# Expert weights in 2 MB units with 16 KB runs per partition, eight slots in place of sixteen

## What is computed

```python
def moe_ffn(h, router_w, router_b, w_gate_up, b_gate_up, w_down, b_down):
    logits = (hf @ router_w + router_b).astype(jnp.float32)
    top_vals, top_idx = lax.top_k(logits, TOP_K)          # 4 of 32 experts
    gates = jax.nn.softmax(top_vals, axis=-1)
    ...
    def run_block(args):
        tok, e = args
        xb = h_pad[tok]
        gu = xb @ w_gate_up[e] + b_gate_up[e]             # 1024 -> 2048
        gate = jnp.minimum(gu[:, :EXPERT_DIM], SWIGLU_LIMIT)
        up = jnp.clip(gu[:, EXPERT_DIM:], -SWIGLU_LIMIT, SWIGLU_LIMIT)
        act = gate * jax.nn.sigmoid(SWIGLU_ALPHA * gate) * (up + 1.0)
        return act @ w_down[e] + b_down[e]                # 1024 -> 1024
    ...
    y = jax.ops.segment_sum(out, slot_token, num_segments=n_tok + 1)[:n_tok]
```

## Time and profile before

| | us |
|---|---|
| median of 3 runs | 1174.46 (1172.85 to 1175.27) |
| span of the profiled execution, first to last instruction | 1171.9 |
| PE busy in the span | 1062.5 (91%) |
| first of the 16 pairs: first addition into the output | 286.06 |
| last of the 16 pairs: first addition into the output | 1165.98 |
| DMA engines from 300 us to 1140 us | busy throughout, 418 GB/s |

### The profile page before, as it was taken

How to read it: one execution, slowest core, us unless ns; L and a number is a source line. 1 busy time by engine, 2 the same in 40 slices (tenths; PEclk the granted TensorE clock), 3 DMA queues, 4 the chain that set the end, 5 groups by cost and what they waited for, 6 DMA issues and landing times.

```text
span 1171.9 us, 11745 instructions
## 1 busy us (share of the span) xinstructions
PE 1062.5 (91%) x4392; PEld 409.5 (35%) x4392; DVE 300.4 (26%) x585; ACT 166.6 (14%) x272; POOL 5.2 (0%) x12
## 2 busy tenths in 40 slices
PE   5999999899998989898989898989898989898987
PEld 2444544433333333333333333333333333233322
DVE  1563021322122222222222212121212121222212
ACT  2123200311111111111111101010101010111110
POOL 1000000000000000000000000000000000000000
PEclk9999999899999999999999999999999999999999
DMA  9942322798999999999999999999999999999996
GB/s 329 348 139 98 131 105 110 276 414 352 414 423 413 422 414 421 414 422 415 422 414 422 415 422 415 421 415 422 416 419 417 421 418 418 418 419 418 417 420 255
DMA packets 84019, 430.36 MB, mean 367 GB/s; under 512 B 7953, under 2 KB 8081, under 8 KB 51233
## 3 DMA queue, kind: packets, MB, share of 16 engines
q1 hardware_dynamic: 83456, 428.20, 90.0%
q0 software_dynamic: 544, 1.90, 0.5%
HBM read 429.03 MB, written 1.05 MB: 367 GB/s over the span
## 4 chain that ended last, share of the span: by engine, by line
PE 63%; SPq 25%; issue 3%; DMA 3%; DVE 3%; ACT 1%; DVEq 0%; PEldq 0%
SPq L262 25%; PE bank L1029 24%; PE bank L1083 13%; PE bank L826 9%; PE bank L848 5%; PE bank L992 4%; PE bank L1098 3%; DMA ring<-w_gate_up_dram 2%; PE bank L998 2%; DVE big L758 2%; DMA ring<-w_in_dram 1%; ACT big L419 1%; PE bank L801 1%; DVE big L776 1%; ACT big L436 1%
## 5 line engine op out<-in xcount | busy, mean ns | idle before, releaser
L1029 PE MATMUL bank<-ring,big 128*64 128x512 f32 x1536 | 342.6, 596 | 8.9 <-PE bank L1029 5.6
L1029 PEld LDWEIGHTS bank<-ring,big 128*64 128x64 f32 x1536 | 107.2, 137 | 229.1 <-issue 212.8
L1083 PE MATMUL bank<-ring,big 128*64 128x512 f32 x768 | 168.3, 594 | 0.0
L826 PE MATMUL bank<-ring,hT 128*128 128x512 f32 (+1 forms) x256 | 105.3, 570 | 4.6 <-DMA ring<-w_in_dram 4.0
L751 DVE COPY big<-bank 128x512 f32<-128x512 f32 x32 | 22.1, 691 | 304.7 <-PEq L1042 177.5
L1083 PEld LDWEIGHTS bank<-ring,big 128*64 128x64 f32 x768 | 53.8, 137 | 103.1 <-issue 103.1
L992 PE MATMUL bank<-xn,kqT 128*128 128x512 f32 x136 | 65.9, 629 | 19.0 <-DVE big L758 19.0
L436 ACT ACTIVATE big<-bank 128x512 f32<-128x512 f32 x32 | 19.1, 597 | 410.2 <-PEq L1042 270.3
L998 PE MATMUL bank<-consts,big 128*128 128x128 f32 x392 | 52.8, 277 | 26.8 <-ACT big L436 14.1
L1098 PE MATMUL bank<-big,kqT 128*128 128x512 f32 x128 | 61.8, 615 | 15.3 <-DVE big L776 15.3
L826 PEld LDWEIGHTS bank<-ring,hT 128*128 128x128 f32 x256 | 47.0, 196 | 60.0 <-issue 60.0
(11 more groups left out here) (216 smaller groups left out, 699.7 us busy)
## 6 DMA issues: line engine op xcount, KB each, us to landing
ring<-w_gate_up_dram SPq DMA_DIRECT2D x192, 1024.0 KB, 19.6
ring<-w_down_dram SPq DMA_DIRECT2D x96, 1024.0 KB, 20.5
siga<-w_gate_up_dram SPq DMA_DIRECT2D x16, 1024.0 KB, 22.1
sigp<-w_gate_up_dram SPq DMA_DIRECT2D x16, 1024.0 KB, 24.1
qo<-w_gate_up_dram SPq DMA_DIRECT2D x16, 1024.0 KB, 23.4
hT<-w_gate_up_dram SPq DMA_DIRECT2D x16, 1024.0 KB, 24.8
ring<-w_in_dram SPq DMA_DIRECT2D x14, 1024.0 KB, 14.4
siga<-w_down_dram SPq DMA_DIRECT2D x8, 1024.0 KB, 21.3
```

The costliest lines, as they stand in the source:

```text
L826: ins = MM(bank[PAIR_BANKS[j % 3][b]][:, 0:n], hT[:, kc, b * P:b * P + P], w[:, k, :], start=kc == 0, stop=kc == KC - 1)
L1029: ins = MM(bank[2 * e + h][T * g:T * g + T, :], xgT[:, k, T * e:T * e + T], ring[s][:, D * g + 512 * h:D * g + 512 * h + 512], start=k == ...
L1083: ins = MM(bank[4 + h][T * e:T * e + T, :], actT[:, c, T * e:T * e + T], v3(ring[ws[e]][:, :], 2)[:, k, 512 * h:512 * h + 512], start=c == ...
```

## The change

A unit becomes 2 MB, with one run of 16 KB for each partition: two neighbouring rows of gate/up, or four of down. A pair has 12 units, 8 of gate/up and 4 of down. There are 8 slots with the same bytes in all: six of the `ring`, one that joins `siga` and `sigp` (`sg`), one that joins `hT` and `qo` (`hq`). The front part uses the ring as 12 halves with their own semaphores, as before; the loop's slots get new ones (`slot_in`, `slot_used`).

With `k` rows to a partition, partition `p` now holds rows `k p` to `k p + k - 1`. So the operands that meet the weights are rearranged: the transposes of the gathered tokens (`X`) take every second column of their source, and those of the gate/up result (`TA`, `TB`) every fourth. The two tables on partitions are rearranged once, on the chip: a new function `turn_tables` on PE between `projection(0)` and `projection(1)` multiplies them with columns of the identity into two PSUM banks, and DVE copies them from there to `bgu` and a new tile `g2`; PE waits for that copy.

```diff
-RING = 12
-EXTRA = 4
+RING = 6
+EXTRA = 2
 SLOTS = RING + EXTRA
+HALVES = 2 * RING
-PAIR_UNITS = 24
-UW = 2048
+PAIR_UNITS = 12
+UW = 4096
+HW = 2048
...
-        ring += [siga_t, sigp_t, qo_t, hT_t]
+        half = [ring[s // 2][:, HW * (s % 2):HW * (s % 2) + HW] for s in range(HALVES)]
+        ring += [sg_t, hq_t]
...
-            if u < 16:
-                row = (2 * p + u // 8) * D + (u % 8) * P
-                return w_gu[bass.ds(row, P), :]
-            j = u - 16
-            row = (2 * p + j % 2) * D + (j // 2) * 2 * P
-            return w_dn[bass.ds(row, 2 * P), :].rearrange("(k p) n -> p k n", p=P)
+            if u < 8:
+                row = (2 * p + u // 4) * D + (u % 4) * 2 * P
+                return w_gu[bass.ds(row, 2 * P), :].rearrange("(p k) n -> p (k n)", k=2)
+            j = u - 8
+            row = (2 * p + j % 2) * D + (j // 2) * 4 * P
+            return w_dn[bass.ds(row, 4 * P), :].rearrange("(p k) n -> p (k n)", k=4)
...
                 if s < RING:
-                    sp.wait_ge(unit_used[s], PRE_TURNS)
+                    sp.wait_ge(unit_used[2 * s], PRE_TURNS)
+                    sp.wait_ge(unit_used[2 * s + 1], PRE_TURNS)
                 elif s == RING:
                     sp.wait_ge(t_ready, TJ_M + 4)
-                elif s == RING + 2:
-                    sp.wait_ge(job_ready, 2 * (BJ_WA + NB))
-                elif s == RING + 3:
+                else:
                     sp.wait_ge(t_ready, TJ_R[1] + 1)
                 pair_unit(0, s)
...
+            dve.wait_ge(turned_ready, 1)
+            V.tensor_copy(bgu_t[:, :].rearrange("p (e j k g) -> p e j k g", e=E, j=2, k=4),
+                          bank[4][:, :].rearrange("p (k e j g) -> p e j k g", k=4, e=E, j=2)).then_inc(turned_read, 1)
+            V.tensor_copy(g2_t[:, :].rearrange("p (j k) -> p j k", k=2), bank[5][:, 0:KC].rearrange("p (k j) -> p j k", k=2)).then_inc(turned_read, 1)
+            dve.wait_ge(turned_read, 2)
...
+            def turn_tables():
+                pe.wait_ge(bgu_in, 16)
+                pe.wait_ge(cols_in, 16)
+                for k in range(4):
+                    for g in range(4):
+                        MM(bank[4][32 * g:32 * g + 32, k * P:k * P + P], ident[:, k::4],
+                           bgu_t[:, :].rearrange("p (e j c g) -> p e j c g", e=E, j=2, c=4)[:, :, :, g, :],
+                           start=True, stop=True)
+                for k in range(2):
+                    for g in range(2):
+                        ins = MM(bank[5][64 * g:64 * g + 64, 4 * k:4 * k + 4], ident[:, k::2], cols[:, P_G2 + g:P_G2 + g + 7:2],
+                                 start=True, stop=True)
+                ins.then_inc(turned_ready, 1)
+                pe.wait_ge(turned_read, 2)
+
             for j in range(4):
                 projection(j)
+                if j == 0:
+                    turn_tables()
...
-            def turn(name, src, h):
+            def turn(name, src, h, rows):
                 for k in range(4):
                     c = 4 * h + k
-                    ins = nc.tensor.transpose(TB[h][:, k * P:k * P + P], src[:, c * P:c * P + P], ident)
+                    c0 = c // rows * rows * P + c % rows
+                    ins = nc.tensor.transpose(TB[h][:, k * P:k * P + P], src[:, c0:c0 + rows * (P - 1) + 1:rows], ident)
                 ins.then_inc(done[f"{name}{h}"], 1)
...
-                    s = landed(8 * e + k)
+                    s = landed(4 * e + k // 2)
...
-                    ins.then_inc(unit_used[s], 1)
+                    if k % 2 == 1:
+                        ins.then_inc(slot_used[s], 1)
...
-                    turn("TA", gu_sb, h)
+                    turn("TA", gu_sb, h, 4)
...
-                    turn("X", xg, h)
+                    turn("X", xg, h, 2)
...
-                for k2 in range(KC // 2):
+                for k2 in range(KC // 4):
```

More of the change, by code:

```diff
@@ L162, in block_kernel @@
         TB = [bank[6], bank[7]]
-        unit_in = [sem(f"unit_in{s}") for s in range(SLOTS)]
-        unit_used = [sem(f"unit_used{s}") for s in range(SLOTS)]
+        unit_in = [sem(f"unit_in{s}") for s in range(HALVES)]
+        unit_used = [sem(f"unit_used{s}") for s in range(HALVES)]
+        slot_in = [sem(f"slot_in{s}") for s in range(SLOTS)]
+        slot_used = [sem(f"slot_used{s}") for s in range(SLOTS)]
+        bgu_in, turned_ready, turned_read = sem("bgu_in"), sem("turned_ready"), sem("turned_read")
         x_in = [sem("x_in0"), sem("x_in1")]
@@ L244, in _ @@
             sp.dma_start(x[:, 1, :], x_d[P:2 * P, :]).then_inc(x_in[1], 16)
-            for s in range(RING, SLOTS):
-                sp.sem_inc(unit_in[s], 16 * PRE_TURNS)
             def pre_unit(u):
-                s = u % RING
-                if u >= RING:
-                    sp.wait_ge(unit_used[s], u // RING)
+                s = u % HALVES
+                if u >= HALVES:
+                    sp.wait_ge(unit_used[s], u // HALVES)
                 src, w = pre_unit_src(u)
                 k = 4 if u < 16 else 2
-                sp.dma_start(v3(ring[s][:, 0:w], k), src).then_inc(unit_in[s], 16)
+                sp.dma_start(v3(half[s][:, 0:w], k), src).then_inc(unit_in[s], 16)
             def pair_unit(p, v):
                 s, u = v % SLOTS, v % PAIR_UNITS
-                dst = ring[s][:, :] if u < 16 else v3(ring[s][:, :], 2)
                 src = pair_unit_src(p if v < PAIR_UNITS else p + 1, u)
-                sp.dma_start(dst, src).then_inc(unit_in[s], 16)
+                sp.dma_start(ring[s][:, :], src).then_inc(slot_in[s], 16)
             for u in range(PRE_UNITS):
@@ L785, in _ @@
             MM = nc.tensor.matmul
-            for s in range(RING, SLOTS):
-                pe.sem_inc(unit_used[s], PRE_TURNS)
+            for s in range(SLOTS):
+                pe.sem_inc(slot_used[s], LEAD)
             tj = [0]
@@ L804, in unit @@
             def unit(u):
[L805 to L807 removed]
+                s = u % HALVES
+                pe.wait_ge(unit_in[s], 16 * (u // HALVES + 1))
+                return half[s]
             def free_unit(u, ins):
[L810 removed]
+                ins.then_inc(unit_used[u % HALVES], 1)
             def free_banks(j):
@@ L1074, in pair_step @@
                 pe.wait_ge(d_copied[1], c1)
-                for k2 in range(KC // 2):
+                for k2 in range(KC // 4):
                     ws = []
                     for e in range(2):
-                        ws.append(landed(16 + 2 * k2 + e))
-                    for k in range(2):
-                        c = 2 * k2 + k
+                        ws.append(landed(8 + 2 * k2 + e))
+                    for k in range(4):
+                        c = 4 * k2 + k
                         for h in range(2):
@@ L1111, in two_pairs @@
             def two_pairs(count, it, with_bias):
-                turns = [count(3 * it + (t + 1 + PRE_TURNS)) for t in range(3)]
-                turns_in = [count(48 * it + 16 * (t + 1 + PRE_TURNS)) for t in range(3)]
+                turns = [count(3 * it + (t + 1 + LEAD)) for t in range(3)]
+                turns_in = [count(48 * it + 16 * (t + 1)) for t in range(3)]
                 for half in range(2):
```

53 lines of the change are left out of this document (26 added, 27 removed).

## The result

The changed kernel takes 1181.51 us (median of 4 runs, 1179.05 to 1183.18), where the kernel before took 1174.69 beside it. The ratio is 1.0061, 95% interval 1.0041 to 1.0082: **slower by 0.6%**, where I forecast faster by 0.4%. The profiled execution spans 1181.4 us against 1171.9, 9.5 more.

The account below looks back on a forecast made before the run. PE was taken to bound the first eleven pairs, the DMA the last four. Loop -8.2 and tables +3.5 gave -4.7 on the 1171.9 us span, 1167.2; with the median 2.6 above, 1169.8 us, range 1167 to 1185.

Parts of the forecast that it names:

- the three signs of being wrong: Eight transposes above 1.06 us, DMA rate under 424 GB/s, or clock drops in the loop without waits for weights.
- What bounds the kernel now: Loop: PE bounds eleven pairs at 58.11 us each; then slots run dry and DMA sets the last four, 60.2.
- point 1: Weight DMA: 16 KB runs reach 428 GB/s, so a pair needs 58.8 us of DMA instead of 60.2.
- point 2: Loop: PE no longer waits for weights, 4.4 MB lost of 8 usable; all pairs 58.11 us, 8.2 us less.
- point 3: Front part: turning the tables between two projection groups costs PE 3.5 us more, between 2.2 and 6.
- point 5: Loop's transposes: stepped weight loads cost nothing; the upper bound, half pace, is 14.6 us over sixteen pairs.
- rival A: Loop's transposes: stepped loads are slow, at half pace +9.9 us, so 1184.4; chance 0.30.

Follow-up runs that it names:

- contig: The changed kernel with the transposes TA, TB and X reading columns side by side again, output not the reference's: 1171.71 us, ratio 0.9985.
- runs8: The changed kernel's 2 MB units and eight slots, but old 8 KB and 4 KB runs and old rows, so no steps or tables: 1183.17 us, ratio 1.0086.
- both: The changed kernel without the stepped columns and without the turned tables, output not the reference's: 1167.06 us, ratio 0.9944.
- perm2: The changed kernel with the step moved from the transposes to the ACT and DVE copies, which read PSUM with it: 1172.67 us (one time).
- best1: The changed kernel with the step read by the copies from PSUM and the tables turned in the router's stage: 1166.6 us, ratio 0.9938.
- pad3: The changed kernel with plain columns and one transpose more in the first half of TA, TB and X in each pair: 1181.9 us, ratio 1.0077.
- the filler: Four matmuls more per pair in PE's waits around the gather, result unread; added to the changed kernel: 1176.59 us, ratio 1.0034.

## Why the prediction was wrong, point by point

Two of the three signs of being wrong that I had named came: the eight transposes take 1.20 us, more than 1.06, and the clock drops in the loop without any wait for weights. That 1181.5 lies inside the stated range of 1167 to 1185 is luck: the range went that far up only for stepped loads at half pace, and they cost a fifth of that.

- **What bounds the kernel now**: right. PE's pair of 58.11 us and the dry slots of the last four account for the loop of before, and contig shows them apart: 871.7 without the waits, as worked out.
- **Longer runs** (point 1): right. 428 GB/s forecast from the line through 2, 4 and 8 KB, 428 measured; runs8 shows that it is the run.
- **The loop** (point 2): right in itself, 8.2 us less in contig and both; perm2 and best1, with the same pair, had one clock drop in the loop and so 6.5 less. The usable lead was a little smaller, 7 MB instead of 8, still above the 4.4 needed.
- **The tables** (point 3): 3.5 forecast, 2.6 measured for work and wait (the products took 1.6, of the 2.3 I had given them). But the sum ended with the last of these rows. The clock dropped behind the tables in each of the seven profiles that have them there: 3.2 more. The three differences elsewhere in the front part, -0.8, -1.7 and +2.6, add 0.1 between them, and it is 6.0 in all.
- **Columns with a step** (point 5): the step that failed first. I took nothing, between bounds of nothing and 14.6. A load costs 0.02 us more, about a fifth of the 0.107 of half pace; each group of eight takes 0.14 longer, and with what DVE's waits take back that is 0.32 us a pair, 4.8 in fifteen. It isn't the step of four against the step of two either: the rule on 16-byte lines that I had set beside it from the Trainium skill (Advanced Engine Details and Errata, SBUF Cachelines) would charge the one and spare the other, and here both pay the same.
- **What was missing**: nothing in the sum or among the rivals said that a pair longer by half a percent can bring the clock down. I had put the only drop of the old loop down to the waits before it, and so counted 1.7 us as gained with them, although pair 13 had waits of 0.26 to 0.58 us for weights at 954 to 959 us too, and its gather took 3.67; "the clock drops without a wait for weights" stood only in the list of what would make me wrong. It was 7.0 us in the profile, the largest of the terms that I hadn't counted, and pad3 shows that it needs no stepped load and no wait for weights.

The account: -8.2 + 4.8 + 7.0 + 6.0 = +9.6 us, against 9.5 in the spans. It is that of the profiled executions. The mean granted clock says the same of the timed ones: it averages 0.9875 over the change's four and 0.993 over the 49 of the kernel before, which over some 1180 us makes an estimated 7 us of full clock lost, and the medians differ by 6.8. My rival A had the right sign and half of the cause, but its price was half pace for each load; the loads' own cost with the forecast's 3.5 for the tables, -8.2 + 4.8 + 3.5, would have ended at no change. What made the kernel slower is the clock.

## What to carry to other kernels

When a permutation has to be made somewhere, put it where an engine reads PSUM: there it was free, as PE's stationary operand it made eight loads take 1.04 instead of 0.86 us, as a write to SBUF it about doubled a copy. In a loop that repeats the same short waits of PE, count a change of the pair's length as a risk of its own, look at the gather-like stretches of several pairs, not one, and fill the waits with matmuls nobody reads if the clock drops there. A one-time step on PE belongs where PE waits anyway, not between two groups of matmuls.

## What was not expected of the hardware

- The clock drop repeats with the loop: every 235.5 us, four pairs, in the changed kernel. In the profiles there were none or one in fifteen pairs at 58.11 us, three or four at 58.43, and none at 58.43 with the filler.
- A stepped load of 128 columns takes 209 ns instead of 140 in the records, but in a row of eight only 0.02 us more each, and a step of two costs what a step of four does.
- ACT and DVE read every fourth float of PSUM at full pace (597 and 691 ns), and write SBUF with 512 bytes between floats at about half (1272 and 1258).
- The DMA rate follows the length of the contiguous run up to 16 KB: 387, 410, 422 and 428 GB/s for 2, 4, 8 and 16 KB; twice the bytes per DMA with the same runs change nothing (417 in runs8, 418 before).
